# Linear attention's score products load only the causal keys of each 16-query sub-block

## The chip, the cores and the metric

The kernel runs on one core of a Trainium2 chip. Five engines work side by side, each through its own queue: TensorE (PE in the rows, with its weight loads as PEld), VectorE (DVE), ScalarE (ACT), GpSimd (POOL) and SyncE (SP, which here only issues transfers). They wait for each other on semaphores. TensorE multiplies a stationary operand (loaded first, up to 128 columns) with a moving operand that streams through it, and writes to PSUM, eight banks of 512 fp32 words in each of 128 partitions. The metric is the device time of one launch in microseconds (us), median of the runs; lower is better.

## The reference

Two blocks for 512 tokens of width 1024. The first is a mixer of convolutions with a mixture-of-experts layer (PEER) whose rows are gathered; the second has a gated linear attention layer, a latent attention layer and two gated feed-forward layers. The change is in the gated linear attention (4 heads, key width 128, value width 256):

```
def gla_chunked(q, k, v, log_a):
    """Causal gated linear attention, chunk-wise form.
    q,k,log_a (B,S,H,DK), v (B,S,H,DV) -> (B,S,H,DV).
    S_t = diag(a_t) S_{t-1} + k_t^T v_t ; o_t = q_t S_t."""
    ...
        diff = b[:, :, :, None, :] - b[:, :, None, :, :]
        decay = jnp.exp(jnp.where(causal, diff, -jnp.inf))
        attn = jnp.einsum('bhik,bhjk,bhijk->bhij', qi, ki, decay)
        o_intra = jnp.einsum('bhij,bhjv->bhiv', attn, vi)
```

Here `b` is the running sum of the log decay in a chunk. A score of query i and key j is a product over 128 features with a decay of its own for each feature, and is zero where j is after i.

## The kernel before

The whole program is written out by hand, one instruction stream for each engine; what an engine waits for is a semaphore count (`need`, `wait_ge`), and nothing is reordered. All matmuls of the stage in question are fp32, and the trace has two records, each a weight load and a matmul, for one fp32 matmul of the program.

The kernel takes linear attention in chunks of 128 tokens, so there are 16 pairs of head and chunk (`GLA_G`, index `g`). The scores of one pair are a 128 x 128 tile, keys on the partitions and queries along the columns, and the 16 tiles fill banks 4 to 7. The decay is taken about a reference point of each sub-block of 16 queries (`GLA_SUB`): for sub-block i VectorE forms differences into `kd` (`k_diff`, L2710), ScalarE takes the exponential (L2007, L2027), and VectorE multiplies by the keys (L2724, semaphore `k_sub`). `kd` has two halves, used in turn, and `k_diff(i)` waits for the products of sub-block i - 2 (`amat_done`). Only the first 16 (i + 1) keys are formed, since the later ones lie after every query of the sub-block.

TensorE then makes for each of the 8 sub-blocks 16 matmuls (L1193), one for each `g`: the stationary operand is all 128 keys of `kd`, the moving one 16 queries. Where `kd` holds no formed keys it holds zeros, which GpSimd wrote once before the stage (L1537). Between two sub-blocks TensorE makes one chunk of the projection `r` (L1202): 8 matmuls of 512 moving columns with weights from `wring`, which SyncE fetches in units of two chunks. ScalarE evicts each chunk (L2030).

After the eighth sub-block VectorE multiplies the banks with the causal mask `keep` (L2731), which makes `amat`; TensorE transposes `gtmp2` into the same banks (L1211), and products with values and states follow (L1225, L1229, L1232), then the output projection `gla_out` on split operands (L656, L660, L664), for which GpSimd prepares the weights (L1479, L1485), and the feed-forward layer.

Ahead of the stage VectorE works off the gate: evicts it with L2693, subtracts (L2696), scans (L2698), forms differences (L2701, L2704, L2710), while TensorE makes the projections for q and k (L602) and v (L613).

Of the kernel before, what the change touches and what calls it, by code (L numbers as in the profile page):

```python
# [19 lines left out]
P = 128  # L20
# [80 lines left out]
def build(nc, A, out):  # L101
    with ExitStack() as ctx:
        S = {n: ctx.enter_context(nc.semaphore(n)) for n in SEMS}
        S.update({name: S[of] for name, (of, _) in AGAIN.items()})
        w_landed = [ctx.enter_context(nc.semaphore(f"w_landed{i}")) for i in range(2)]
        ada_landed = [ctx.enter_context(nc.semaphore(f"ada_landed{i}")) for i in range(2)]
# [66 lines left out]
        ps = ctx.enter_context(nc.psum_tensor("ps", [P, 8, 512], F32))  # L173
# [26 lines left out]
        def col(name, k=0, n=1):  # L200
            _, tile, r0, _ = vectors[name]
            return par[:, tile, r0 + k:r0 + k + n]
# [132 lines left out]
        qsub = R.take(GLA_H, T)  # L335
# [6 lines left out]
        kd = work[:, :, :].rearrange("p (a c) k -> p a (c k)", a=2)  # L342
# [37 lines left out]
        def gsubs(x):  # L380

            return x.rearrange("p h (t k) -> p (h t) k", k=P)

        def kd_g(a):
            return kd[:, a, :].rearrange("p (g k) -> p g k", g=GLA_G)
# [167 lines left out]
        def _(e):  # L553
# [5 lines left out]
            def need(name, n):  # L559
                n += FROM.get(name, 0)  # L560
                c[name].at = max(c[name].at, n)
                e.wait_ge(S[name], n)

            def inc(ins, name, n=1):
                ins.then_inc(S[name], n)
                c[name].add(n)
# [6 lines left out]
            def slot(kc, width=UNIT, n=16):  # L573

                u = st["u"]
                st["u"] += 1
                landed[u % 2].add(n)
                e.wait_ge(landed[u % 2].sem, landed[u % 2].value())
                return wring[:, u % 2, 0:kc * width].rearrange("p (k n) -> p k n", n=width)
# [147 lines left out]
            def nrhs(k):  # L727
                return nT[:, k, :]
# [3 lines left out]
            for t in range(TT):  # L732
                e.wait_ge(x_landed[t], 16)
                for half in range(2):
                    i = 2 * t + half
                    if i >= 4:
                        need("hT_in", i - 3)
                    for q in range(4):
                        mm = e.transpose(ps[:, 4 + i % 4, q * P:(q + 1) * P], x_tok[:, t, (4 * half + q) * P:(4 * half + q + 1) * P],
                                         ident[:])  # L740
# [128 lines left out]
            def out_matmul(w, bank, j, k, first, last):  # L869

                return e.matmul(bank, w[:, k, j * P:(j + 1) * P], mixT[:, k, :], start=first, stop=last)  # L871
# [16 lines left out]
            for m in range(4):  # L888
                for k in range(3):
                    if m == 0:  # L890
                        mixed(k)
                    mm = out_matmul(held[m // 2], banks[m], m % 2, k, False, k == 2)
                inc(mm, "chunk_done")
                dve.add()
            for g in range(2):
                w = slot(DC)
                for j in range(2):
                    e.wait_ge(dve.sem, dve.value(3))
                    for k in range(DC):
                        mm = out_matmul(w, banks[2 * g + j], j, k, k == 0, k == DC - 1)  # L900
# [76 lines left out]
            def first_matmul(w, bank, j, k):  # L977

                return e.matmul(ps[:, bank, 0:P], w[:, k, j * P:(j + 1) * P], nT[:, k, 0:P], start=(k == 0), stop=(k == DC - 1))
# [30 lines left out]
            for k in range(DC):  # L1010
                fresh(k)
                for j in range(2):
                    mm = first_matmul(w0, j, j, k)
            inc(mm, "q_first")
            w1 = slot(DC)
            for j in range(2):
                for k in range(DC):
                    mm = first_matmul(w1, 2 + j, j, k)
# [132 lines left out]
            for u in range(4):  # L1151
# [3 lines left out]
                for k in range(DC):  # L1155
                    if u == 0 and k % 4 == 0:
                        need("last_norm", k // 4 + 1)
                    mm = e.matmul(ps[:, (2, 3, 0, 1)[u], 0:UNIT], nT[:, k, late], w[:, k, :],
                                  start=(k == 0), stop=(k == DC - 1))
# [11 lines left out]
            for k in range(DC):  # L1171
                if k == 0:
                    need("last_x", 2)
                mm = e.matmul(ps[0:16, 5, :], wglr[:, k, :], nT[:, k, :], start=(k == 0), stop=(k == DC - 1))
# [3 lines left out]
            for h in range(GLA_H):  # L1178
                mm = e.matmul(ps[:, 4 + h, :], wgate[0:16, h * P:(h + 1) * P], glrT[0:16, :], start=True, stop=True)
# [9 lines left out]
            r_first = st["u"]  # L1189
            for i in range(8):  # L1190
                need("k_sub", i + 1)
                for g in range(GLA_G):
                    mm = e.matmul(ps[:, 4 + g // 4, (g % 4) * P + 16 * i:(g % 4) * P + 16 * i + 16],  # L1193
                                  kd_g(i % 2)[:, g, :], gsubs(qsub)[:, g, 16 * i:16 * i + 16], start=True, stop=True)
                inc(mm, "amat_done")

                j = i % 2
                if j == 0:
                    w = slot(DC)
                e.wait_ge(act.sem, act.value(3))  # L1200
                for k in range(DC):
                    mm = e.matmul(ps[:, 2 * ((i // 2 + r_first) % 2) + j, :], w[:, k, j * P:(j + 1) * P], nrhs(k),  # L1202
                                  start=(k == 0), stop=(k == DC - 1))
                inc(mm, "chunk_done")
                act.add()
            settle()
            need("kw_ready", 1)
            for h in range(GLA_H):
                need("a_ready", h + 1)
                for t in range(TT):  # L1210
                    mm = e.transpose(ps[:, 4 + h, t * P:(t + 1) * P], gtmp2[:, h, t * P:(t + 1) * P], ident[:])  # L1211
                inc(mm, "kw_t")
            need("ew_done", 1)
            for t in range(TT):
                for h in range(GLA_H):
                    i = t * GLA_H + h
                    g = h * TT + t
# [6 lines left out]
                    for v in range(2):  # L1224
                        mm = e.matmul(ps[:, b, v * P:(v + 1) * P],  # L1225
                                      gvt[:, t, h * GLA_DV + v * P:h * GLA_DV + (v + 1) * P], amat[:, g, :],
                                      start=True, stop=(t == 0))
                        if t:
                            mm = e.matmul(ps[:, b, v * P:(v + 1) * P], state[:, h, v * P:(v + 1) * P],  # L1229
                                          gq[:, h, t * P:(t + 1) * P], start=False, stop=True)  # L1230
                    if t < TT - 1:
                        mm = e.matmul(ps[:, b, 2 * P:4 * P], kwt[:, g, :], gvt[:, t, h * GLA_DV:(h + 1) * GLA_DV],  # L1232
                                      start=True, stop=True)
# [70 lines left out]
            for m in range(4):  # L1304
                w = slot(3, width=384, n=64)
                for j in range(3):
                    e.wait_ge(act.sem, act.value(3))
                    for k in range(3):
                        mm = e.matmul(ps[:, (base + 3 * m + j) % 4, :], w[:, k, j * P:(j + 1) * P], cT6[:, k, :],  # L1309
                                      start=(k == 0), stop=(k == 2))  # L1310
# [6 lines left out]
            for u in range(2):  # L1317
                w = slot(2, width=4 * (NOPE + VDIM))
                for i in range(8):
                    bank = ps[:, (base + 8 * u + i) % 4, :]  # L1320
                    e.wait_ge(act.sem, act.value(3))
                    for k in range(2):
                        if i < 4:
                            at = i * (NOPE + VDIM)
                            mm = e.matmul(bank, w[:, k, at:at + NOPE], cT6[:, 3 + k, :], start=(k == 0), stop=(k == 1))
                        else:
                            t = i - 4
                            values = w[:, k, :].rearrange("p (h c) -> p h c", c=NOPE + VDIM)[:, :, NOPE:NOPE + VDIM]
                            mm = e.matmul(bank.rearrange("p (h c) -> p h c", c=VDIM), cT6[:, 3 + k, t * P:(t + 1) * P], values,
                                          start=(k == 0), stop=(k == 1))  # L1330
# [55 lines left out]
            for half in range(2):  # L1386
                for t in range(TT):
                    i = TT * half + t
                    if i >= 3:
                        need("fin_ready", i - 2)  # L1390
                    for k in range(4):
                        if t == 0:
                            last(half * 4 + k)
                        mm = e.transpose(ps[:, 5 + i % 3, k * P:(k + 1) * P], nT[:, half * 4 + k, t * P:(t + 1) * P],
                                         ident[:])
# [4 lines left out]
        def _(e):  # L1400
            k = Count(S["pl_ch"])

            def chain(ins):
                ins.then_inc(k.sem, 1)
                k.add()
                e.wait_ge(k.sem, k.value())
# [127 lines left out]
            chain(e.memset(reset, 1.0))  # L1534
            for t in range(TT):
                chain(e.memset(reset[:, t * P:t * P + 1], 0.0))
            e.memset(kd, 0.0).then_inc(S["consts"], 1)  # L1537
            e.wait_ge(S["last_norm"], FROM["last_norm"] + 6)
            ada(1)

# [659 lines left out]
        def _(e):  # L2200
# [4 lines left out]
            def need(name, n):  # L2205
                n += FROM.get(name, 0)
                c[name].at = max(c[name].at, n)
                e.wait_ge(S[name], n)

            def inc(ins, name):  # L2210
                ins.then_inc(S[name], 1)
                c[name].add()

            def own(ins, name="v_ch"):

                inc(ins, name)
                e.wait_ge(S[name], c[name].value())
# [476 lines left out]
            need("glog_l", 1)  # L2694
            need("consts", 3)
            own(e.tensor_tensor(gtmp, gb, gtmp2, ALU.subtract))  # L2696
            for h in range(GLA_H):
                own(e.tensor_tensor_scan(gb[:, h, :], reset, gtmp[:, h, :], 0.0, ALU.mult, ALU.add))  # L2698

# [21 lines left out]
            for i in range(8):  # L2721
                n = 16 * (i + 1)
# [139 lines left out]
            for i in range(MLA_H * TT):  # L2862
                if i + 2 < MLA_H * TT:
                    peak(i + 2)
                n = (i % TT + 1) * P
# [41 lines left out]
```

## Time and profile before

| | us |
|---|---|
| device time, median of 3 runs | 3100.79 (3098.17 to 3100.93) |
| span of the profiled execution, first to last instruction | 2955.2 |
| profiled execution's own time: its span and what lies around it; no separate total is recorded, and the median less the span is | 145.6 |
| TensorE busy in the span | 2668.3 (90%) |
| TensorE's mean granted clock in the span | 0.957 |
| GpSimd busy | 1651.3 (56%) |
| VectorE busy | 1462.7 (49%) |
| ScalarE busy | 628.6 (21%) |
| all matmuls of L1193, busy | 30.2 |

A granted clock of 1.00 is 2.4 GHz and one of 0.50 is 1.2 GHz; a value between them is a stretch in which both occurred. Busy time of overlapping instructions is counted once. An idle time in brackets stands with what released the engine. The end of a matmul record is modelled, so the distance from one start to the next says more than its duration.

### The profile page before, as it was taken

Reading aid. Unit: us, or ns where it says so; the run is one execution under the profiler, and the core shown is the slowest. Engines: PE = TensorE matmul, PEld = TensorE weight load, DVE = VectorE, ACT = ScalarE, POOL = GpSimd, SP = SyncE. Lnnn points to the kernel's source line nnn. Section 1 sums busy time; section 2 is a strip of 40 time slices with the busy share of each in tenths; the row PEclk is TensorE's granted clock in tenths of the full one; section 3 lists DMA queues with packets and bytes.
Section 4 is the critical chain, followed back from the end, with each engine's and each line's share of the span. In section 5 each row is a group of like instructions: output and inputs, shape, how many; then the busy total and the mean of one; then the engine's idle time right before and its main releaser. Section 6 shows DMA issues by size and latency. Waiting matters only on the chain.

```text
span 2955.2 us, 26705 instructions
## 1 busy us (share of the span) xinstructions
PE 2668.3 (90%) x8997; PEld 1630.8 (55%) x8997; DVE 1462.7 (49%) x3275; ACT 628.6 (21%) x1324; POOL 1651.3 (56%) x1273
## 2 busy tenths in 40 slices
PE   8999998877887787778998999999999998899998
PEld 7744443333333333333444476778888744688887
DVE  6867666666666666667653412445234525311111
ACT  2222221222122122221223211421100223211101
POOL 5306667767776777767773680256555301256663
PEclk9999999988998999999999999999999999999999
DMA  6339999999999999999996451145345220132232
GB/s 209 114 114 387 405 406 409 408 383 409 409 407 390 405 409 409 409 384 409 404 409 251 145 168 43 43 142 190 108 155 188 81 81 0 57 99 91 94 107 78
DMA packets 325193, 725.19 MB, mean 245 GB/s; under 512 B 24868, under 2 KB 187602, under 8 KB 325090
## 3 DMA queue, kind: packets, MB, share of 16 engines
q0 software_dynamic: 150720, 549.52, 47.1%
q1 hardware_dynamic: 136930, 136.64, 14.4%
q10 hardware_dynamic: 37440, 37.75, 4.0%
q8 instruction: 53, 0.87, 0.1%
q14 instruction: 50, 0.41, 0.0%
HBM read 721.74 MB, written 2.10 MB: 245 GB/s over the span
## 4 chain that ended last, share of the span: by engine, by line
PE 62%; DMA 14%; POOL 11%; issue 5%; DVE 4%; ACT 2%; SPq 0%; POOLq 0%; DVEq 0%; ACTq 0%
PE ps L958 13%; DMA arena<-in_expert_u_dram,arena 10%; PE ps L664 10%; PE ps L660 10%; PE ps L656 9%; POOL arena L1508 8%; POOL work L1508 3%; PE ps L922 3%; PE ps L1202 2%; PE ps L602 2%; PE ps L613 2%; PE ps L871 2%; DMA work<-in_expert_u_dram,arena 1%; DVE ps L2365 1%; PE ps L1309 1%
## 5 line engine op out<-in xcount | busy, mean ns | idle before, releaser
L958 PE MATMUL ps<-arena 128*128 128x512 f32 x1536 | 754.0, 635 | 196.4 <-ACT arena L1816 127.0
L958 PEld LDWEIGHTS ps<-arena 128*128 128x128 f32 x1536 | 301.6, 203 | 605.1 <-issue 497.6
L2580 DVE CUSTOM_DVE_ANT_0 arena<-arena,ps 128x1024 f32<-128x1024 f32 x384 | 468.1, 1220 | 328.8 <-DMA arena<-in_expert_u_dram,arena 319.2
L1508 POOL DMA_INDIRECT arena<-in_expert_v_dram,arena x384 | 360.5, 939 | 197.5 <-PE ps L958 103.3
L1508 POOL DMA_INDIRECT arena<-in_expert_u_dram,arena x384 | 361.7, 942 | 137.8 <-issue 98.5
L1485 POOL TENSOR_TENSOR wlo<-wring,whi_f 128x2048 fp32r<-128x2048 f32 (+1 forms) x60 | 302.9, 5048 | 22.5 <-DVE n_lo L2686 11.9
L1479 POOL TENSOR_SCALAR whi_f<-wring 128x2048 fp32r<-128x2048 f32 (+1 forms) x60 | 125.3, 2089 | 288.8 <-DMA wring<-in_ffn_w_in_dram 170.0
L958 PE MATMUL ps<-work,arena 128*128 128x512 f32 x512 | 239.0, 600 | 19.6 <-DMA work<-in_expert_v_dram,arena 19.6
L660 PE MATMUL ps<-n_hi,wlo 128*128 128x512 f32 x1024 | 255.4, 392 | 0.7 <-POOL wlo L1485 0.5
L660 PEld LDWEIGHTS ps<-n_hi,wlo 128*128 128x128 f32 x1024 | 191.9, 188 | 43.7 <-POOL wlo L1485 2.3
L2580 DVE CUSTOM_DVE_ANT_0 work<-work,ps 128x1024 f32<-128x1024 f32 x128 | 156.3, 1221 | 104.8 <-DMA work<-in_expert_u_dram,arena 104.8
L2778 DVE TENSOR_TENSOR arena<-ps,arena 128x512 f32 (+1 forms) x44 | 30.4, 692 | 354.8 <-PE ps L664 354.8
L1816 ACT ACTIVATE arena<-ident,arena 128x128 f32<-128x128 f32 x512 | 153.1, 387 | 237.9 <-DVE arena L2594 235.7
L958 PEld LDWEIGHTS ps<-work,arena 128*128 128x128 f32 x512 | 94.3, 190 | 149.7 <-issue 94.1
L656 PE MATMUL ps<-n_hi,whi_f 128*128 128x512 f32 x704 | 170.0, 395 | 6.0 <-ACT n_hi L1655 6.0
L664 PE MATMUL ps<-n_lo,whi_f 128*128 128x512 f32 x704 | 174.9, 390 | 0.4 <-DVE n_lo L2686 0.3
L656 PEld LDWEIGHTS ps<-n_hi,whi_f 128*128 128x128 f32 x704 | 134.1, 191 | 35.8 <-issue 7.6
L664 PEld LDWEIGHTS ps<-n_lo,whi_f 128*128 128x128 f32 x704 | 132.2, 188 | 29.0 <-DVE n_lo L2686 1.7
L1508 POOL DMA_INDIRECT work<-in_expert_u_dram,arena x128 | 120.6, 942 | 39.1 <-issue 32.3
L1508 POOL DMA_INDIRECT work<-in_expert_v_dram,arena x128 | 120.0, 937 | 39.7 <-issue 35.1
L2266 DVE SCALAR_TENSOR_TENSOR hT<-ps,mod,hT 128x512 f32<-128x512 f32 x32 | 24.0, 751 | 232.2 <-PE ps L664 232.2
L1479 POOL TENSOR_SCALAR whi_m<-wring 128x2048 fp32r<-128x2048 f32 x7 | 13.3, 1901 | 188.2 <-DMA wring<-in_mla_w_out_dram 177.6
(392 smaller groups left out, 3664.2 us busy)
## 6 DMA issues: line engine op xcount, KB each, us to landing
wring<-in_ffn_w_in_dram SPq DMA_DIRECT2D x44, 1024.0 KB, 5.1
arena<-in_ada_w_dram ACTq DMA_DIRECT2D x24, 1024.0 KB, 5.3
wring<-in_ffn_w_out_dram SPq DMA_DIRECT2D x16, 1408.0 KB, 6.4
wring<-in_gla_w_in_dram SPq DMA_DIRECT2D x12, 1024.0 KB, 5.5
arena<-in_ada_w_dram POOLq DMA_DIRECT2D x12, 1024.0 KB, 5.9
work<-in_ada_w_dram ACTq DMA_DIRECT2D x12, 1024.0 KB, 5.3
wring<-in_w_in_dram SPq DMA_DIRECT2D x9, 1024.0 KB, 5.9
wring<-in_w_q_dram SPq DMA_DIRECT2D x8, 1024.0 KB, 16.7
```

What stands on the lines that cost most here:

```text
L602: mm = e.matmul(ps[:, b, :], w[:, k, j * P:(j + 1) * P], rhs(k), start=(k == 0), stop=(k == kc - 1))
L613: mm = e.matmul(ps[:, st_bank + j, q * UNIT:(q + 1) * UNIT], src[:, k, (2 * j + q) * P:(2 * j + q + 1) * P], w[:, k, :], start=(k == 0), s ...
L656: e.matmul(banks[j], wh[:, k, cols[j]], hi(k), start=(start and k == 0), stop=False)
L660: e.matmul(banks[j], wl[:, k, cols[j]], hi(k), start=False, stop=False)
L664: mm = e.matmul(banks[j], wh[:, k, cols[j]], lo(k), start=False, stop=(stop and k == kc - 1))
L922: mm = e.matmul(ps[:, j, :], w[:, k, j * P:(j + 1) * P], nrhs(k), start=(k == 0), stop=(k == DC - 1))
L958: mm = e.matmul(ps[:, 6 + q, :], diag[:, k, :], slot_of(s)[:, q * 512:(q + 1) * 512], start=first, stop=last)
L1479: e.tensor_scalar(hi, w, 1.0, 0.0, ALU.mult, ALU.add).then_inc(w_split.sem, 1)
L1485: e.tensor_tensor(wlo[:, q, 0:kc * UNIT], w, hi.bitcast(F32), ALU.subtract).then_inc(S["w_lo"], 1)
L1508: e.indirect_dma_start(slot_of(seq), None, table, bass.IndirectOffsetOnAxis(ap=idx_flat[:, n * TOPK + k:n * TOPK + k + 1], axis=0)).then_i ...
L1816: inc(e.activation(diag[:, k, :], ident[:], ACT.Copy, scale=coef[:, n % 2, k:k + 1]), "diag_ready")
L2580: inc(e.tensor_tensor_reduce(slot_of(s), slot_of(s), ps[:, 4:6, :].rearrange("p a k -> p (a k)"), 1.0, 0.0, ALU.mult, ALU.add, dots[:, n % ...
```

## The change

The stationary operand of sub-block i is cut to its first `n = 16 (i + 1)` keys, and the output to the same n partitions. Partitions n to 127 of those columns are then not written by TensorE, so VectorE writes zeros to all of banks 4 to 7 before. The zeroing of `kd` by GpSimd goes; its semaphore is still raised.

```
@@ TensorE
             for i in range(8):
                 need("k_sub", i + 1)
+                n = 16 * (i + 1)
                 for g in range(GLA_G):
-                    mm = e.matmul(ps[:, 4 + g // 4, (g % 4) * P + 16 * i:(g % 4) * P + 16 * i + 16],
-                                  kd_g(i % 2)[:, g, :], gsubs(qsub)[:, g, 16 * i:16 * i + 16], start=True, stop=True)
+                    mm = e.matmul(ps[0:n, 4 + g // 4, (g % 4) * P + 16 * i:(g % 4) * P + n],
+                                  kd_g(i % 2)[:, g, 0:n], gsubs(qsub)[:, g, 16 * i:n], start=True, stop=True)
                 inc(mm, "amat_done")
@@ GpSimd
-            e.memset(kd, 0.0).then_inc(S["consts"], 1)
+            e.sem_inc(S["consts"], 1)
@@ VectorE
             need("consts", 3)
             own(e.tensor_tensor(gtmp, gb, gtmp2, ALU.subtract))
+            own(e.memset(ps[:, 4:8, :], 0.0))
             for h in range(GLA_H):
                 own(e.tensor_tensor_scan(gb[:, h, :], reset, gtmp[:, h, :], 0.0, ALU.mult, ALU.add))
```

On TensorE, from the last products of the v projection on, the queue of before reads (the shape is that of the output: its partitions, which are the stationary columns, x the moving columns; x16 is sixteen matmuls of the program):

```order
L613 MATMUL ps<-wring,nT 128x256 x128
L1193 MATMUL ps<-arena,work 128x16 x16
L1202 MATMUL ps<-nT,wring 128x512 x8
L1193 MATMUL ps<-arena,work 128x16 x16
L1202 MATMUL ps<-nT,wring 128x512 x8
```

and that of the change (its lines are one further down):

```order
L613 MATMUL ps<-wring,nT 128x256 x128
L1194 MATMUL ps<-arena,work 16x16 x16
L1203 MATMUL ps<-nT,wring 128x512 x8
L1194 MATMUL ps<-arena,work 32x16 x16
L1203 MATMUL ps<-nT,wring 128x512 x8
L1194 MATMUL ps<-arena,work 48x16 x16
L1203 MATMUL ps<-nT,wring 128x512 x8
L1194 MATMUL ps<-arena,work 64x16 x16
```

Nothing has moved; the stationary columns go from 16 to 128 in steps of 16.

On VectorE, where the gate is worked off, before:

```order
L2693 TENSOR_SCALAR arena<-ps,par 128x512 x4
L2696 TENSOR_TENSOR arena<-arena 128x2048
L2698 SCALAR_TENSOR_TENSOR arena<-arena 128x512 x4
L2701 TENSOR_TENSOR arena<-arena 128x2048
L2704 TENSOR_TENSOR arena<-arena 128x2048
```

and with the change:

```order
L2694 TENSOR_SCALAR arena<-ps,par 128x512 x4
L2697 TENSOR_TENSOR arena<-arena 128x2048
L2698 MEMSET ps 128x2048
L2700 SCALAR_TENSOR_TENSOR arena<-arena 128x512 x4
L2703 TENSOR_TENSOR arena<-arena 128x2048
L2706 TENSOR_TENSOR arena<-arena 128x2048
```

One instruction is new, ahead of the four scans (L2698 before, L2700 after).

## Rows read from the trace of the kernel before

**Rows 1.** The page: span, and busy time of each engine.

```profile
span 2955.2 us, 26705 instructions
PE 2668.3 (90%) x8997; PEld 1630.8 (55%) x8997; DVE 1462.7 (49%) x3275; ACT 628.6 (21%) x1324; POOL 1651.3 (56%) x1273
```

**Rows 2.** Chain that ended last, in order of time: start, length, what.

```profile
1766.76 0.61 ACT arena L2017
1767.40 4.71 PE ps L1193 x32
1772.11 9.35 PE ps L1202 x16
1781.46 3.48 PE ps L1193 x32
1784.94 6.96 PE ps L1202 x16
...
1847.58 8.67 PE ps L1202 x16
1856.28 0.61 ACT arena L2030
```

**Rows 3.** Busy time by stretch, TensorE: length, busy (records), granted clock, DMA.

```profile
1769.90:1776.80 6.90, 6.90 (x18) 0.51 0.24 84
1776.80:1848.40 71.60, 71.60 (x334) 1.00 0.14 45
1848.40:1851.90 3.50, 3.50 (x6) 0.51 0.00 0
```

**Rows 4.** Line L1193's weight loads: ns min/median/max, first and last start.

```profile
L1193 PEld LDWEIGHTS ps<-arena,work x256: 186/192/334, 1767.4 to 1847.3; 128*128 128x128 f32 x128
```

**Rows 5.** Groups by form, narrower weight loads: busy us, mean ns, idle before.

```profile
L819 PEld LDWEIGHTS ps<-arena 128*64 128x64 f32 x48 | 3.7, 135 | 0.7 <-issue 0.7
L1174 PEld LDWEIGHTS ps<-nT,arena 128*16 128x16 f32 x16 | 1.5, 96 | 5.6 <-issue 5.6
```

**Rows 6.** Timeline, two loads in a row, of 128, 64 and 16 columns.

```profile
1781.30 0.30 PEld L1193 LDWEIGHTS ps<-arena,work 128*128 128x128 f32 x2 [0.24 <-issue]
...
126.20 0.19 PEld L819 LDWEIGHTS ps<-arena 128*64 128x64 f32 x2 [0.37 <-issue]
...
1642.16 0.12 PEld L1174 LDWEIGHTS ps<-nT,arena 128*16 128x16 f32 x2 [0.94 <-issue]
```

**Rows 7.** Timeline of weight loads: a whole run of 64-column ones.

```profile
126.20 2.33 PEld L819 LDWEIGHTS ps<-arena 128*64 128x64 f32 x32 [0.37 <-issue]
128.70 0.19 PEld L660 LDWEIGHTS ps<-n_hi,wlo 128*128 128x128 f32 x1 [0.17 <-issue]
```

**Rows 8.** Timeline in latent attention: half-height loads (64*128) between full ones.

```profile
2432.24 0.29 PEld L1348 LDWEIGHTS ps<-arena 64*128 64x128 f32 x2
...
2432.66 0.30 PEld L1347 LDWEIGHTS ps<-arena 128*128 128x128 f32 x2
```

**Rows 9.** Timeline of VectorE ahead of the stage.

```profile
1678.93 3.24 DVE L2704 TENSOR_TENSOR arena<-arena 128x2048 f32<-128x2048 f32 x1
...
1712.98 2.29 DVE L2717 TENSOR_TENSOR arena<-arena 128x2048 f32<-128x2048 f32 x1 [29.22 <-ACT arena L2003]
```

**Rows 10.** Timeline of GpSimd: the zeroing of kd, and what comes after.

```profile
1606.41 3.51 POOL L1537 MEMSET work<- 128x4096 f32 x1
1640.65 1.88 POOL L1436 DMA_DIRECT2D arena<-in_ada_w_dram  x2 [30.73 <-DVE nT L2668]
```

**Rows 11.** Timeline after sub-block 5's products, VectorE and ScalarE on kd.

```profile
1826.81 2.29 DVE L2710 TENSOR_TENSOR work<-arena 128x2048 f32<-128x2048 f32 x1 [6.62 <-PE ps L1193]
...
1829.13 1.91 ACT L2027 ACTIVATE work<-work 128x2048 f32<-128x2048 f32 x1 [5.28 <-DVE work L2710]
1829.13 4.35 DVE L2724 TENSOR_TENSOR work<-work,arena 128x1792 f32<-128x1792 f32 x2
```

**Rows 12.** Timeline of VectorE: the masking after the last sub-block.

```profile
1847.69 2.87 DVE L2731 TENSOR_TENSOR arena<-ps,arena 128x512 f32<-128x512 f32 x4 [14.21 <-PE ps L1193]
```

More of the change, by code:

```diff
@@ L1191, in _ @@
                 need("k_sub", i + 1)
+                n = 16 * (i + 1)
                 for g in range(GLA_G):
-                    mm = e.matmul(ps[:, 4 + g // 4, (g % 4) * P + 16 * i:(g % 4) * P + 16 * i + 16],
-                                  kd_g(i % 2)[:, g, :], gsubs(qsub)[:, g, 16 * i:16 * i + 16], start=True, stop=True)
+                    mm = e.matmul(ps[0:n, 4 + g // 4, (g % 4) * P + 16 * i:(g % 4) * P + n],
+                                  kd_g(i % 2)[:, g, 0:n], gsubs(qsub)[:, g, 16 * i:n], start=True, stop=True)
                 inc(mm, "amat_done")
@@ L1536, in _ @@
                 chain(e.memset(reset[:, t * P:t * P + 1], 0.0))
-            e.memset(kd, 0.0).then_inc(S["consts"], 1)
+            e.sem_inc(S["consts"], 1)
             e.wait_ge(S["last_norm"], FROM["last_norm"] + 6)
@@ L2696, in _ @@
             own(e.tensor_tensor(gtmp, gb, gtmp2, ALU.subtract))
+            own(e.memset(ps[:, 4:8, :], 0.0))
             for h in range(GLA_H):
```

## The prediction

> **What bounds the kernel now.** I begin with the page [rows 1]: TensorE is busy for 90% of the span, no other engine for more than 56%. A share over the whole span does not price one stage, so next comes the chain that ended last, read in order of time around the stage [rows 2]. From 1767.40 to 1856.28 it holds only TensorE: sub-block products (L1193) and projection chunks (L1202) in turn, with no wait between. What TensorE spends there is what the stage takes, 88.9 us. In steady state a pair takes 3.48 + 6.96 = 10.44 us. Two places differ: the first pair takes 4.71 + 9.35 = 14.06, which is 3.62 more, and the last chunk takes 8.67, which is 1.71 more. The stretches [rows 3] say why: the granted clock is 0.51 from 1769.9 to 1776.8 and from 1848.4 to 1851.9, and 1.00 in the 71.6 us between. So the stage is 8 x 10.44 = 83.5 us of work at full clock and 5.3 us paid for a clock of 1.2 GHz.
>
> Inside a run of L1193, 32 records in 3.48 us are 109 ns apart. Of that 16 moving columns can hardly be the reason: two weight loads in a row take 0.30 us together [rows 6] and one takes 192 ns [rows 4], so a load starts 0.11 us after the one before. The runs go at the pace of their weight loads, and the moving operand hides under them.
>
> **The change part by part.**
>
> *Narrower stationary operands.* Loads of fewer columns occur elsewhere: 135 ns for 64 columns, 96 ns for 16 [rows 5]. From 192 that is 0.89 ns a column down to 64 and 0.81 from there to 16; over all (192 - 96) / 112 = 0.86 ns. The start-to-start distance falls too: 0.19 - 0.135 = 0.055 us at 64 columns and 0.12 - 0.096, about 0.03, at 16 [rows 6]. The last is more than 0.86 x 16 = 14 ns, so I take 30 ns as the least distance. With 109 - 0.86 (128 - n), and not below 30, the distances are 30, 30, 40, 54, 68, 82, 95, 109 ns for n = 16 to 128. Against 109 each, 32 records save 2.53, 2.53, 2.20, 1.76, 1.32, 0.88, 0.44 and 0 us: together 11.7 us.
>
> *A price that the diff doesn't show.* In latent attention, where loads of half the height alternate with full ones, two records that start at 2432.24 are followed by the next load at 2432.66 [rows 8], 0.42 us where two full ones need 2 x 0.109 = 0.22. The row after a run of 64-column loads has 0.17 us of idle before it and the one at its start 0.37, both put down to no other engine [rows 7]. So I charge 0.2 us each time that TensorE goes from one size of tile to another. Sub-blocks of 16, 32, 48 and 64 columns stand between chunks of 128, which is 8 such turns: 1.6 us. I assume that 80, 96 and 112 columns count as full; no row shows them, and if they pay as well it is 1.2 us more. The Trainium skill (TensorEngine Tiling (Array Packing), Key Properties) has the rule behind this, which speaks against the change: changing the tiling mode drains TensorE, changing only the tile does not. By that rule alone, without a price, the turns could not be summed; the trace agrees and gives the 0.2 us.
>
> *The clock.* Before the first sub-block TensorE waits for one eviction (0.61 us, [rows 2]), and then come 3.5 us in which little streams; the clock falls inside that run, 2.5 us after its start [rows 3]. With the change the first run is 32 x 0.03 = 1.0 us and full-width chunks follow at once. Six runs of 3.48 us that stand between full chunks did not lower the clock, and one of 3.48, the last, did. A thin stretch of 0.6 + 1.0 + 0.4 us, wait, run and turns, is shorter than any of these, so I take the first fall as gone: 3.6 us. The last run keeps its 128 columns and its 3.48 us, so I leave its 1.7 us in. Bounds: nothing gained, and both gained, 5.3 us.
>
> *VectorE's zeroing of four banks.* 2048 words in each partition. The nearest rows of VectorE at that size take 2.29 and 3.24 us [rows 9]; I take 2 to 3.3 us. It stands ahead of the scans, which end in `dq_ready` and in L2704 at about 1682. What needs them is ScalarE's L2003, which VectorE then awaits for 29.22 us [rows 9], since ScalarE is still evicting q and k. A delay of 3 us is under that cover ten times over: 0 us. Without it the price would be the whole 2 to 3.3 us. TensorE writes these banks next in sub-block 0, behind `q_sub`, which VectorE makes later in its own order.
>
> *GpSimd's zeroing of kd goes.* 3.51 us, after which GpSimd stands for 30.73 us until VectorE's L2668 releases it [rows 10]. Nobody gets anything from it: 0 us.
>
> *What comes closer.* A shorter run brings forward what frees `kd`, and the next run as well, so the question is whether `kd` is ready. After sub-block 5's products VectorE needs 2.29 us for the difference of sub-block 7 and about 1.8 for multiplying sub-block 6, ScalarE 1.91 beside it [rows 11]. That is 0.3 + 2.3 + 1.8 = 4.4 us after the products, and the chunk behind them takes 6.96. The chunk isn't shortened, so 2.5 us stay over at the widest sub-blocks. The masking after the end (2.87 us [rows 12]) fits under the last chunk too. The weights of r, the conversion of `gla_out` by GpSimd and all that follows are released by these same products and chunks, so the gain passes on whole.
>
> **The sum.** -11.7 + 1.6 - 3.6 = -13.7 us. On the profiled execution the span goes from 2955.2 to 2941.5. Around a span lie 145.6 us up to the median of the runs, on which nothing here acts, so I forecast 3100.8 - 13.7 = 3087.1 us.
>
> **The rivals.**
>
> 1. *The clock stays as it was*: the fall only moves to another place in the stage. The last run, which dropped the clock without any wait ahead of it, speaks for this, and the six which didn't speak against. Gain 11.7 - 1.6 = 10.1, time 3090.7 us.
>
> 2. *A least distance that is set by something other than columns.* The run of 32 64-column records takes 2.50 us from first load to the next full one [rows 7], 78 ns each, though with a 128-column moving operand and turns inside. If 78 held for every small record, the seven shorter runs would save 32 x (5 x 31 + 27 + 14) = 6.3 us, less 1.6, so 4.7; with the clock 8.3: 3092.5 us, without it 3096.1. Against it are the 0.055 and 0.03 us between two loads [rows 6], but those are single pairs. The Trainium skill (TensorE: Matmul & The Clock Gate, Wait — 56ns, not 53.3ns?) names such a floor: about 62 ns per matmul where firmware decodes it. With 62 in the same sum it would be 3090.1 us by an estimate from that page; loads 0.055 us apart don't agree with it, and no run here yet shows a long row of small records.
>
> 3. *The narrow form does nothing*: the pace stays 109 ns because the chip takes a full-width slot for each load of a dense run. Then only the turns remain, +1.6, with or without the clock: 3098.8 to 3102.4. The 64-column run at 78 speaks against it.
>
> 4. *Slower, through the clock.* Runs in which ever fewer columns are loaded and 16 stream, with two drains around them, may look idle to what grants the clock. At full clock the changed stage is 83.5 - 10.1 = 73.4 us. A fall as long as the first one costs 3.6 us. All eight runs with one would add 28.8, so 102.2 us, 13.3 more than now: 3114.1 us. It decides at five falls, where 91.4 us passes the 88.9 of now; from seven on (98.6) it is more than 0.2% slower. For it: the last run fell with nothing idle near it. Against it: six equal ones did not, and the thin stretches all get shorter.
>
> **How the numbers follow.** The forecast has 0.56, rival 1 0.18, rival 2 0.14 (most of it with the clock gained), rival 3 0.07, rival 4 0.05. The range: at the low end no price for turns and both falls gone, -17.0, which is 3083.8, and a little for falls of the clock elsewhere after the stage, whose places move with it: 3082. At the high end rival 2 without the clock, 3096. Outside are rival 4 and most of rival 3. 0.2% (6.2 us) is about what a measurement of this kernel tells from no change, so the line is 3094.6 us: faster 0.86 (the forecast, rival 1 and rival 2 with the clock), within 0.09, slower 0.05.
>
> **What the changed profile would show.** The runs of L1194 in the chain should be about 1.0, 1.0, 1.3, 1.7, 2.2, 2.6, 3.0 and 3.5 us, and the step from each of the first four to its chunk about 0.2 us longer. Equal runs of 3.5 would be rival 3, a common length of 2.5 for the first five rival 2. The first chunk should take 6.96 and not 9.35, with a granted clock of 1.00 from 1767 on; if it is 0.5 somewhere in the stage, rival 1 or 4. MEMSET on VectorE should stand in front of a wait on L2003 that has shrunk from 29.2 to some 27 us. The forecast is wrong if a `k_sub` or weight transfer turns up as TensorE's releaser between runs, or if the clock in the stage is not what decides the remainder but falls elsewhere in the span.

## The result

The changed kernel takes 3075.97 us (median of 10 runs, 3066.03 to 3089.39) against 3099.48 us (3084.07 to 3108.2, 10 runs). The ratio is 0.9933, 95% interval 0.9910 to 0.9956: faster by 20.8 us, between 13.6 and 27.9; the medians themselves lie 23.5 us apart, and the text goes by the ratio. The forecast was 3087.1 us in a range of 3082 to 3096, a gain of 13.7. The direction was right and the time lies below the range; the gain is half as large again as forecast, and the 13.7 us lie at the very edge of the interval.

The stage first, in the chain that ended last of the changed kernel, in order of time (start, length, what). It answers to [rows 2].

```profile
1916.41 0.96 PE ps L1194 x32
1917.38 7.06 PE ps L1203 x16
1924.44 1.11 PE ps L1194 x32
...
1932.62 1.54 PE ps L1194 x32
...
1941.23 1.97 PE ps L1194 x32
...
1950.26 2.24 PE ps L1194 x32
1952.50 6.96 PE ps L1203 x16
1959.46 2.65 PE ps L1194 x32
...
1969.07 3.06 PE ps L1194 x32
...
1979.10 3.48 PE ps L1194 x32
1982.58 6.98 PE ps L1203 x16
...
1989.58 0.61 ACT arena L2031
```

A run is the 32 records of one sub-block's 16 matmuls, a chunk the 16 records of one part of `r`. The reader sees runs that grow from 0.96 to 3.48 us where all had 3.48, chunks of 7.06 behind the four narrowest and 6.96 behind the others, and the eviction behind the last chunk. The whole chain has no wait between. From the first product to the last eviction it is 1989.58 - 1916.41 = 73.17 us, where [rows 2] give 88.88: 15.7 us less. The granted clock of the whole stage (stretch, length, busy, clock, DMA) answers to [rows 3]:

```profile
1916.40:1989.60 73.20, 73.13 (x384) 1.00 0.18 58
```

Both falls of the clock (stretches at 1.2 GHz) that [rows 3] show are absent here. VectorE's new instruction and the wait behind it, on its timeline, answer to [rows 9]:

```profile
1810.90 1.76 DVE L2698 MEMSET ps<- 128x2048 f32 x1 [0.50 <-DVE arena L2697]
...
1861.99 4.81 DVE L2719 TENSOR_TENSOR arena<-arena 128x2048 f32<-128x2048 f32 x1 [24.48 <-ACT arena L2004]
```

Its row has 1.76 us, but from the end of the row before it to the start of the one behind it are 2.30 us, where before they are 0.04; so it delays VectorE by about 2.3 us. That disappears in the wait on ScalarE, which is still 24.48 us.

One thing must be read with care: this profile's span is 3085.3 us and not 2955.2 less something.

```profile
span 3085.3 us, 26706 instructions
...
L958 PE MATMUL ps<-arena x1536: 592/592/1222, 296.8 to 1743.8; 128*128 128x512 f32 x192
```

The second row is the first and last start of a group of the expert layer, which the change does not touch: 1447 us from one to the other. Both kernels come in two such lengths, by the chip on which they run, and in the first profile of before the same group takes 1333 us. Below, the kernel before has 2960.94 us with a span of 2959.3 on one chip, and medians of 3096 to 3098 us on two others. The changed kernel's profiled execution took 3086.93 us. So a span is 1.6 us shorter than its time. Only ratios from one chip, and stages, are compared from here on.

Between these two profiles the stage accounts for 15.7 of 20.8 us. Whether the missing 5 lie outside it, or the first profile of before showed a short stage by chance, is what the experiments had to tell.

### The profile page after: what moved, and what is told of

Same layout as the page of the kernel before. It is cut to its first block, busy times and chain, and to the rows that moved or that the text cites. A ratio compares the mean times of both kernels' runs of the same rounds, so it can differ in the third digit from the quotient of the medians.

```text
span 3085.3 us, 26706 instructions
## 1 busy us (share of the span) xinstructions
PE 2683.3 (87%) x8997; PEld 1625.6 (53%) x8997; DVE 1463.9 (47%) x3276; ACT 629.7 (20%) x1324; POOL 1650.2 (53%) x1272
## 3 DMA queue, kind: packets, MB, share of 16 engines
q1 hardware_dynamic: 136930, 136.64, 13.8%
## 4 chain that ended last, share of the span: by engine, by line
PE 67%; issue 8%; POOL 7%; DMA 7%; DVE 5%; another core or an unknown queue 4%; ACT 2%; SPq 0%; ACTq 0%; POOLq 0%; DVEq 0%
PE ps L958 18%; PE ps L660 9%; PE ps L664 9%; PE ps L656 9%; POOL arena L1509 5%; PE ps L922 3%; DMA arena<-in_expert_u_dram,arena 2%; PE ps L602 2%; PE ps L1203 2%; PE ps L613 2%; POOL work L1509 2%; PE ps L871 1%; DMA arena<-in_expert_v_dram,arena 1%; PE ps L1081 1%
## 5 line engine op out<-in xcount | busy, mean ns | idle before, releaser
L958 PE MATMUL ps<-arena 128*128 128x512 f32 x1536 | 769.6, 645 | 273.5 <-issue 121.4
L1486 POOL TENSOR_TENSOR wlo<-wring,whi_f 128x2048 fp32r<-128x2048 f32 (+1 forms) x60 | 303.0, 5049 | 22.5 <-DVE n_lo L2687 11.9
L958 PE MATMUL ps<-work,arena 128*128 128x512 f32 x512 | 243.7, 609 | 20.8 <-DMA work<-in_expert_v_dram,arena 12.7
```

Source lines behind the costliest of these rows:

```text
L958: mm = e.matmul(ps[:, 6 + q, :], diag[:, k, :], slot_of(s)[:, q * 512:(q + 1) * 512], start=first, stop=last)
L1486: e.tensor_tensor(wlo[:, q, 0:kc * UNIT], w, hi.bitcast(F32), ALU.subtract).then_inc(S["w_lo"], 1)
```

## Experiments

All times of a stage are from the start of the first product to that of the last eviction, in the chain. Where a kernel has wider loads than the change, GpSimd's zeroing of `kd` stays, so that the keys that are not formed count as zeros; VectorE's zeroing stays too. But for the two kinds with more moving columns, every sub-block still streams its own 16 queries; the cuts shown give only the line with the widths.

**The kernel before, three more times.** No edit.

> The kernel before, unchanged, against itself, to have a second profile of it and the width of the measurement. Theory (the whole gain lies in the stage of the sub-blocks, 15.7 us): the stage takes 83.5 us of work at full clock and 2 to 6 us for falls of the clock, so 85 to 90 us from the first product of sub-block 0 to the eviction of the last chunk; the ratio is 1.000 and its interval 0.3 to 0.5% wide. Rival (something outside the stage gave the rest of the 23.5 us between the medians): another profile of this kernel shows the stretches outside the stage longer than the changed kernel's by some 8 us, the same in every profile.

> The kernel before once more, for a third profile of its stage. Theory (the part of the gain beyond loads and turns is falls of the clock that the first profile happened to have few of): work 83.5 us plus falls, so 87 to 98 us, with the excess over 83.5 equal to half of the time that the clock is at 1.2 GHz in the stage. Rival (the second profile with 97.9 was the exception): 89 us again with a fall at the start and one at the end.

> The kernel before, a fourth profile of its stage; the same expectations as for the third. If the mean of the four stages is 92 to 96 us, the changed kernel's 73 to 74 accounts for the 20.7 us by which the rounds differ; if it is 90 or less, 4 us of them stay open.

Against itself the kernel measures 0.9996 (0.9985 to 1.0008). Its second profile, the chain in the stage:

```profile
1768.30 4.20 PE ps L1193 x32
1772.50 9.88 PE ps L1202 x16
1782.38 4.08 PE ps L1193 x32
1786.46 9.72 PE ps L1202 x16
1796.19 4.21 PE ps L1193 x32
...
1809.99 4.35 PE ps L1193 x32
1814.34 9.44 PE ps L1202 x16
1823.78 3.48 PE ps L1193 x32
1827.26 6.96 PE ps L1202 x16
...
1865.58 0.61 ACT arena L2030
```

and the clock in stretches of it:

```profile
1771.40:1778.20 6.80, 6.80 (x13) 0.50 0.17 59
1778.20:1785.10 6.90, 6.90 (x37) 0.99 0.01 2
1785.10:1791.90 6.80, 6.80 (x14) 0.50 0.00 0
...
1798.70:1805.50 6.80, 6.80 (x15) 0.50 0.35 121
...
1812.40:1819.20 6.80, 6.80 (x16) 0.50 0.00 0
1819.20:1865.00 45.80, 45.80 (x203) 1.00 0.15 47
```

The same instructions as in [rows 2] take 97.28 us. The clock falls four times, each time in a run of L1193, stays down for 6.8 us and is back before the next run, in which it falls again; why the fifth run has no fall isn't shown. Four times half of 6.8 is 13.6, and 97.28 - 83.5 is 13.8. The 85 to 90 us that I had expected was a miss. The third profile has 95.56 us with a mean granted clock of 0.88, the fourth 93.90 with 0.89. With the first, the four stages are 88.88, 97.28, 95.56 and 93.90 us, mean 93.9. The changed kernel's stage is shorter than that by 20.7 us. The first profile was the mildest of four. The rival, a constant surplus outside the stage, isn't seen either: from the last eviction to the end of the program are 1091 to 1099 us in these four profiles and 1090 to 1099 in the three of the change, and up to the first product, on the chips with the short spans, 1767 to 1769 us against 1771 in after_again.

**The changed kernel, two more times.** No edit.

> The changed kernel, unchanged. Theory: the stage takes 73 to 75 us as in its first profile, and the time is 0.4 to 0.6% under the kernel before, 12 to 19 us. Rival: 0.7 to 0.8% under it (21 to 25 us), in both sets of rounds, which would ask for a gain outside the stage.

> The changed kernel on the same chip as the two others of this call. Theory: ratio 0.9930, stage 73.2 us without a fall of the clock, a third profile of that kind. Rival: a fall in one of the long last runs, stage 75 to 77 us.

0.9930 (0.9914 to 0.9945) on the chip of before_again and 0.9932 (0.9910 to 0.9954) on another, with stages of 73.16 us both times and a granted clock of 1.00 throughout. Three profiles without a fall, then. The rate of 0.7% is the rival's number in the expectation of after_again, and the 0.4 to 0.6% of the theory was a miss; the rival's reason, a gain outside the stage, is not what the profiles show.

The timed runs can be asked too, since each has its span and its mean granted clock on record. Half speed for some time costs half of it, so span x (1 - clock) estimates what a run loses to 1.2 GHz anywhere in the program, if TensorE sets the pace there. On the first of the two chips that is 132.7 us on average over 29 runs of the kernel before (clock 0.9551) and 122.4 over six of the change (0.9583): 10.3 us less, give or take 3.4 (95%), of the 20.3 by which the mean spans differ. On the second it is 12.5, give or take 7, of 20.8 (28 and 11 runs). So half of the gain is the clock in unprofiled executions as well.

**VectorE's zeroing alone** (`wide_zero`: 128 columns in all sub-blocks):

```
-                n = 16 * (i + 1)
+                n = (128, 128, 128, 128, 128, 128, 128, 128)[i]
```

> All eight sub-blocks load 128 columns, as in the kernel before, but VectorE zeroes banks 4 to 7 as in the change, and GpSimd zeroes kd as before. Theory (VectorE's zeroing is covered): VectorE's wait on L2004 behind it is 24 to 27 us, TensorE's chain through the q, k and v projections is as long as before, and the stage takes 85 to 90 us. Rival (the zeroing delays or brings forward something): the stretch from the first product for the gate (L1175) to the first sub-block differs by 2 us or more from the kernel before.

One run, 2962.61 us against a median of 2962.04. VectorE's row for the zeroing has 1.76 us, and the wait on L2004 behind it is 23.74 us, where before_again has 29.67. From the first product for the gate to the first sub-block it is 1769.9 - 1644.7 = 125.2 us, as in before_again (1768.3 - 1643.1). The stage takes 97.26 us, with four falls like before_again's, more than the 85 to 90 that I had put down when I knew one profile only. The zeroing costs nothing that these stretches show.

**Sub-block 0 alone, and all but sub-block 0** (`first_only`, `not_first`):

```
+                n = (16, 128, 128, 128, 128, 128, 128, 128)[i]      # first_only
+                n = (128, 32, 48, 64, 80, 96, 112, 128)[i]          # not_first
```

> Only sub-block 0 loads fewer columns (16); the seven others load 128; both zeroings stay. Theory (the first fall of the clock comes from the long thin first run behind a wait): run 0 takes 1.0 us, no fall of the clock begins in it or in its chunk, and the stage takes 83.5 - 2.5 + 0.3 = 81.3 us, plus 1.7 or 3.6 us for each fall that a later 3.5 us run brings. Rival (falls come by chance, wherever the stage begins): a fall begins within 4 us of the start of the stage here too, and the stage takes 85 us or more.

> Sub-block 0 loads 128 columns, the others their causal keys; both zeroings stay. Work at full clock: 73.2 of the changed kernel + 2.5 for the wide run - 0.3 for two turns less = 75.4 us from the first product to the last eviction. Theory (a 3.5 us thin run right behind a wait brings the fall): a fall begins within 4 us of the start, and the stage takes 77 to 79 us. Rival (falls hang on the whole row of runs, not on the first): no fall, 75.4 us.

The end of the stage in first_only:

```profile
1832.93 3.48 PE ps L1194 x32
1836.41 8.66 PE ps L1203 x16
1845.06 4.20 PE ps L1194 x32
1849.26 9.62 PE ps L1203 x16
...
1858.90 0.61 ACT arena L2031
```

and not_first at its start and end:

```profile
1903.74 4.12 PE ps L1194 x32
1907.87 9.96 PE ps L1203 x16
1917.83 1.11 PE ps L1194 x32
...
1962.46 3.44 PE ps L1194 x32
1965.90 9.96 PE ps L1203 x16
1975.86 4.00 PE ps L1194 x32
1979.86 9.82 PE ps L1203 x16
```

With sub-block 0 narrow no fall begins before the seventh chunk; the stage takes 86.2 us, which is 81.1 of work and half of the 10.2 us at 1.2 GHz (3.4 in the seventh chunk, 6.8 from the last run on). With sub-block 0 wide the fall at the start is there (3.2 us after the first product), as it was in all four profiles of before. But the expectation of 77 to 79 us was wrong: two more falls of 6.8 us come in the runs of 112 and 128 columns, and the stage takes 86.0 us. So the long late runs of the change can bring a fall as well; that three profiles show none doesn't exclude it. These are one profile each.

**Widths in steps** (`upto64`, `quadrants`, `from80`):

```
+                n = (16, 32, 48, 64, 128, 128, 128, 128)[i]         # upto64
+                n = (32, 32, 64, 64, 96, 96, 128, 128)[i]           # quadrants
+                n = (80, 80, 80, 80, 80, 96, 112, 128)[i]           # from80
```

> Sub-blocks 0 to 3 load 16 to 64 columns, 4 to 7 load 128; both zeroings stay. At full clock the stage takes runs of 1.0, 1.1, 1.5, 2.0 and four of 3.48, chunks of 7.06 four times and 6.96 four times: 75.6 us. Theory (falls come in 3.5 us runs): falls, if any, only from sub-block 4 on, each 1.7 or 3.4 us; stage 76 to 86 us, and none in the first four. Rival (falls come where the wait is): a fall in the first chunk.

> The widths are rounded up to 32, 32, 64, 64, 96, 96, 128, 128; both zeroings stay. Theory (a load costs 0.83 us per 1000 columns and two turns of 0.15 us for widths up to 64): runs of 1.1, 1.1, 2.0, 2.0, 2.65, 2.65, 3.5, 3.5, stage 74.6 us from first product to last eviction, 1.4 more than the change, none of it from the clock. Rival (widths that are no multiple of 32 pay extra, which these don't): the runs of 64 and 96 columns take under 1.9 and 2.5 us, and the stage no more than the changed kernel's 73.2.

> No sub-block loads fewer than 80 columns: 80 five times, then 96, 112, 128; both zeroings stay. Theory (turns between tile sizes occur only at widths up to 64, and cost 0.3 us for each such run): no chunk takes more than 6.96 us at full clock, the first five runs take 2.24, and the stage 76.1 us plus falls. Rival (the 7.06 us chunks and the longer first step come from narrow outputs, whatever the tile): chunks after 80-column runs take 7.06 too.

quadrants, two of its widths, and from80, the start of its chain:

```profile
1936.18 1.97 PE ps L1194 x32
1938.15 7.06 PE ps L1203 x16
...
1965.55 2.65 PE ps L1194 x32
1968.21 6.96 PE ps L1203 x16
```

```profile
1767.34 2.47 PE ps L1194 x32
1769.80 8.66 PE ps L1203 x16
1778.46 2.24 PE ps L1194 x32
1780.70 6.96 PE ps L1203 x16
```

Stages: 77.3 us (upto64, one fall of 3.4 us, just behind the first 3.5 us run), 76.3 (quadrants, one of 3.4 us at the end of the first 96-column run) and 79.7 (from80, two of 3.4 us, just behind the first run of 80 columns and behind that of 96). So a run needn't be the full 3.5 us for a fall, as upto64's theory had it; but in no profile of any kernel here does one begin in or right behind a run of 64 columns or fewer. A run takes the same at a width of 64 or 96 whether its keys fill it or not. At full clock widths from 80 on have chunks of 6.96 us behind them, widths up to 64 chunks of 7.06, in each of the kernels that stream 16 queries: the turn between tile sizes has a price and is where I put it. It is small beside what it buys: the 16-column run with its turn takes 0.96 + 0.10, the 80-column run 2.24.

**More moving columns under full-width loads** (`thick`, `thick_again`). Each sub-block streams all queries from its own to the end of the chunk, and the later sub-blocks write over what is too much:

```
-                    mm = e.matmul(ps[:, 4 + g // 4, (g % 4) * P + 16 * i:(g % 4) * P + 16 * i + 16],
-                                  kd_g(i % 2)[:, g, :], gsubs(qsub)[:, g, 16 * i:16 * i + 16], start=True, stop=True)
+                    mm = e.matmul(ps[0:n, 4 + g // 4, (g % 4) * P + 16 * i:(g % 4 + 1) * P],
+                                  kd_g(i % 2)[:, g, 0:n], gsubs(qsub)[:, g, 16 * i:P], start=True, stop=True)
```

with n = 128.

> All eight sub-blocks load 128 columns, as before the change, but stream not 16 queries but all from 16 i to the end of the chunk, 128, 112, ... 16 moving columns; the columns that are too many are written again by the sub-block to which they belong. Both zeroings stay. The loads set the pace (two loads 0.11 us apart, and 128 moving columns take no longer elsewhere), so at full clock the stage has the same 83.5 us as before. Theory (the missing part of the gain is falls of the clock, and they come because little streams in the runs): no fall begins in the first runs, where 128 to 64 columns stream, the stage takes 84 to 87 us against 89 to 98 in the kernel before, and the time is 0.2 to 0.4% under it. Rival (the clock falls because of the run's weight loads or of the wait ahead of it, whatever streams): the stage takes 89 to 98 us and the time is that of before.

> Full-width loads with more moving columns, timed a second time, since its first time (0.9984, 0.9964 to 1.0003) did not tell its stage's gain from none. Theory (half of the change's gain is the clock): the stage takes 83.5 to 84 us with no fall, 10 us under the mean of 93.9 us of the four profiles of before, so the ratio is 0.9965, 0.9950 to 0.9980. Rival (what is gained in the stage is given back by falls elsewhere, or the four profiles had more falls than the unprofiled runs): ratio 0.999 to 1.000.

```profile
1918.26 3.84 PE ps L1194 x32
1922.10 6.87 PE ps L1203 x16
1928.97 3.56 PE ps L1194 x32
1932.53 6.88 PE ps L1203 x16
```

The pairs take 10.4 to 10.7 us (10.44 at full clock before), with the same weight loads and behind the same wait; and the clock is 1.00 in the whole stage:

```profile
1918.30:2002.00 83.70, 83.70 (x384) 1.00 0.16 51
```

83.8 us in both of its profiles, no fall, where before and wide_zero, with the same loads, have two to four falls in each of five profiles and one of them always in the first run. So it is how little streams beside the loads that brings the falls; the loads and the wait alone don't. In time it is 0.9984 (0.9964 to 1.0003) and 0.9986 (0.9965 to 1.0007), some 5 us faster, where the difference of stages, 93.9 - 83.8, asks for 10 (0.9967). Neither interval excludes 0.9967, and neither excludes no gain; both times lie between thick_again's theory and its rival. By span x (1 - clock) its runs lose 3.6 us less than before on one chip (give or take 3.6) and 6.7 less on the other (4.3). That is about half of what the stages ask for: either timed runs of thick have falls in the stage that two profiles don't show, or falls come elsewhere in their place. No run here tells which.

**Narrow loads with moving columns as many as are free** (`narrow_thick`, `narrow_thick_b`), the widths of the change and

```
+                m = 16 * i + min(P - 16 * i, n)
```

as the end of the moving and the output columns.

> The changed kernel's widths, and in each sub-block as many moving columns as hide under the load: the smaller of 128 - 16 i and the width, so 16, 32, 48, 64, 64, 48, 32, 16; GpSimd's zeroing is gone as in the change. Theory (streaming keeps the clock up, and moving columns up to the width are free): runs within 0.1 us of the changed kernel's, no fall in the stage, stage 73 to 74 us and time 0.6 to 0.8% under the kernel before, no better than the change, whose stage had no fall either. Rival (moving columns are not free beside narrow loads): the runs of 16 to 64 columns take up to twice as long, stage 76 us or more.

> The changed kernel's widths with as many moving columns as hide, beside the changed kernel on one chip. Theory (no fall is left in the stage to gain): within 0.1% of the changed kernel, 0.9930, stage 73.2 to 73.4 us. Rival (it has something more to gain, as its first time, 0.9915 against 0.9930, may hint): 0.15% or more under the changed kernel on this chip.

0.9915 (0.9897 to 0.9932) and 0.9934 (0.9914 to 0.9954), beside the change's 0.9930 and 0.9932. The runs are at most 0.04 us longer than the change's, so the moving columns are free up to the width of the load. Its stages take 73.2 us without a fall and 74.9 with one of 3.4 us in the last chunk, behind the run in which its moving operand is again 16 columns; I had expected none, so this is a miss. On one chip the two medians are 3080.84 and 3076.92: it has nothing more to give that can be measured.

## Why the prediction failed

**What bounds the kernel** was right for the stage: TensorE is the whole chain before and after, and all of what the stage loses reaches the end. The work at full clock, 8 x 10.44 = 83.5 us, was right too; thick takes 83.8.

**The loads** (11.7 us forecast) and **the turns** (1.6 us back), together 10.1. Measured: the runs save 10.8 us and four chunks give back 0.1 us each, together 10.4. From 128 to 80 columns a run shrinks by 0.41 us for each 16, 0.80 ns a column and record, not 0.86; down to 64, 48 and 32 it is 0.10 to 0.14 us above that line, and the chunk behind is 0.10 longer: a turn costs about 0.1 us each way, where I had charged 0.2. I had the loads' saving somewhat too large and the turns twice too dear, and that the two errors nearly cancel is luck. The least distance is right: 32 records of 16 columns in 0.96 us are 30 ns apart, so rival 2, 78 ns a record, is excluded.

The Trainium skill (TensorE: Matmul & The Clock Gate, Wait — 56ns, not 53.3ns?) has 62 ns per matmul where firmware decodes it. Taken for each record, as in my rival, that is excluded by the 30 ns. Taken for each matmul of the program, of two records, it would be 60 ns here (0.96 us for 16), too near to 62 to exclude, and no run tells the two readings apart.

The Trainium skill (TensorEngine Tiling (Array Packing), Key Properties) says that changing the tiling mode drains TensorE. The trace agrees as far as a price goes, 0.1 us each way at widths up to 64; widths of 80 to 112 count as full.

**The clock** is the term that failed: 3.6 us, with 5.3 as its upper bound. I took the falls of one profiled execution as those of the kernel, and read its six runs without a fall as a sign that such a run does not lower the clock. It does in other executions of the same program: two falls in one, four, four and three in the others, which cost 5.4 to 13.8 us, on average 10.4. (The reading was also a little off: the second fall of that profile begins 0.8 us behind the last run, in its chunk.) The forecast's bound was drawn from the smallest of the four. The changed kernel has no fall in three of three profiles. 10.4 and 10.4 make 20.8 us, the measured gain; that it fits to the decimal is chance, as four stages that spread over 8 us can't give so exact a mean. That the falls come from thin runs was half of my argument; I put the wait before the first run beside it, and thick, with the same wait and no fall, shows that the wait alone doesn't do it.

**Around the span** I had placed 145.6 us "on which nothing here acts". There is no such part: a span is 1.6 us shorter than its time, and the profiled execution, by its span of 2955.2 us and its 1333 us for the expert layer's group, is one of the short kind that two of the chips run, while the timed ones were of the long kind. It did no harm to the difference, but the sentence is false.

**VectorE's zeroing** (0 us under a cover of 29 us): right, about 2.3 us under what is still 24. The wait shrank by 4.7 and not 2.2 us, mostly because the first pair of differences behind it (L2710 before, L2712 now) took 6.46 us in place of 1.56; why isn't shown. It starts TensorE no later: the row behind the wait begins 54.42 us ahead of the first product before and after. **GpSimd's** was idle time before and after: no kernel here took it away by itself, and in the change its 3.51 us went with nothing to be seen for it. **What comes closer**: no `k_sub` and no transfer appears between runs; right.

How the gain divides in unprofiled executions is known roughly. By four profiles the clock's part is 10.4 us; by the granted clock of the timed runs it is 10.3, give or take 3.4, on one chip and 12.5, give or take 7, on another; narrow_thick has 11.9 (5.2) and narrow_thick_b 4.9 (5.3). What stays open is why thick, whose profiles show no fall either, gets back only about 5 of the 10 us, and what makes one full-width run lower the clock and the next one not.

## What to carry to other kernels

A run of fp32 matmuls with a small moving operand goes at the pace of its weight loads, so cutting the stationary operand to what is needed pays in proportion, down to 30 ns a record. TensorE being busy is not the same as the clock staying up: look for stretches in which it mostly loads weights, and shorten them, which here took the falls away with the work. To stream more columns under the same loads cost 0.3 us of stage here and kept the falls away in two profiles, but its gain in time was not clear of noise. And a clock that falls at some places in one execution falls at others in the next: price such a term from several profiles, or bound it by every run of that kind having a fall, not by the falls that one profile happens to show.

## What the runs showed of the hardware

- At a width of 128 columns and 16 moving columns, the clock fell 2 to 3.2 us after the first product in all four profiles of before and in both variants with a wide first run behind the wait (wide_zero, not_first), and stayed down for 6.8 us. Falls of 3.4 us occur too, and all of them begin at the end of a run or up to 1.0 us behind it, as in from80, 3.0 us after its first product.
- 128 moving columns in place of 16 under the same loads cost 0.36 us in the first run of 32 records and 0.08 in the second, with 112; the chunk behind the first was 0.09 us shorter (thick).
- Two chips ran the kernel before in medians of 2962 us and two others in 3096 and 3098; most of the difference is in the expert layer (its matmul group takes 1447 us in after against some 1333 in after_again, with DMA at about 370 against 408 GB/s there), and none in this stage (73.17 and 73.16 us).
- VectorE's row for writing 2048 fp32 words of zeros in each partition of PSUM has 1.76 us (0.86 ns a word), but the rows around it stand 2.30 us apart, against 0.04 without it: 2.26 us, 1.10 ns a word.
